# Gate and up products of 18 of 22 tiles by seven products per 2x2 block, in six feed-forward layers on one core

## What is computed

```
def swiglu(h, w1, w3, w2):
    return (jax.nn.silu(h @ w1) * (h @ w3)) @ w2          # 1024 -> 2816 -> 1024
def swiglu_2(h, w_in, w_out):
    gate, up = jnp.split(h @ w_in, 2, axis=-1)            # 1024 -> 2 x 2816 -> 1024
    return (jax.nn.silu(gate) * up) @ w_out
```

## Time and profile before

| | us |
|---|---|
| median of three runs | 2272.77 |
| lowest, highest | 2272.24, 2274.1 |
| the profiled execution, its own time | 2274.54 |
| its span, first to last instruction | 2272.5 |

### The profile page before, as it was taken

The page is one execution under the profiler, slowest core; times in us unless marked ns, Lnnn a source line. Parts: engine busy times, 40 slices in busy tenths (PEclk is TensorE's granted clock), DMA queues, the critical chain, the costliest instruction groups (busy, mean ns, idle before and its releaser), DMA issues.

```text
span 2272.5 us, 23963 instructions
## 1 busy us (share of the span) xinstructions
PE 2211.6 (97%) x10232; PEld 1871.7 (82%) x10232; DVE 766.8 (34%) x1601; ACT 356.2 (16%) x667; POOL 118.8 (5%) x231
## 2 busy tenths in 40 slices
PE   7999999999999999999999999999999999999997
PEld 4777888868888888888788888888888868888886
DVE  6454333313334122336433422332233543340002
ACT  3233200022000100023140200020002223120001
POOL 0100011100111000100000000000010000000000
PEclk9999999999999999999999999999999999999998
DMA  9673576825767565643434465656564433444331
GB/s 357 226 259 102 213 267 245 311 79 186 270 248 295 220 230 199 254 147 146 162 111 148 157 231 200 236 195 231 213 231 154 154 148 111 148 148 148 137 127 70
DMA packets 61539, 438.27 MB, mean 193 GB/s; under 512 B 6976, under 2 KB 8768, under 8 KB 39552
## 3 DMA queue, kind: packets, MB, share of 16 engines
q1 hardware_dynamic: 28608, 318.35, 38.4%
q0 software_dynamic: 32256, 117.45, 13.9%
q10 hardware_dynamic: 576, 1.05, 0.1%
HBM read 434.72 MB, written 2.10 MB: 192 GB/s over the span
## 4 chain that ended last, share of the span: by engine, by line
PE 97%; DVE 1%; ACT 1%; issue 0%; DMA 0%; SPq 0%; ACTq 0%; DVEq 0%
PE lin L1460 79%; PE small_ps L1460 4%; PE lin L1775 2%; PE lin L1718 1%; PE small_ps L1794 1%; PE lin L1528 1%; PE lin L1732 1%; PE small_ps L1564 1%; PE small_ps L1685 1%; PE lin L1672 1%; PE lin L1740 1%; PE small_ps L1766 0%; PE pstat L1472 0%; PE lin L1600 0%; PE small_ps L1615 0%; PE lin L1587 0%
## 5 line engine op out<-in xcount | busy, mean ns | idle before, releaser
L1460 PE MATMUL lin<-h,ring 128*128 128x256 f32 x5424 | 1180.3, 380 | 5.4 <-ACT h L807 2.8
L1460 PEld LDWEIGHTS lin<-h,ring 128*128 128x128 f32 x5424 | 1030.0, 190 | 150.7 <-issue 9.2
L1460 PE MATMUL lin<-big,ring 128*128 128x256 f32 x2112 | 457.4, 379 | 7.9 <-DVE big L1422 7.9
L1460 PEld LDWEIGHTS lin<-big,ring 128*128 128x128 f32 x2112 | 400.8, 190 | 64.5 <-DVE big L1422 10.3
L871 DVE CUSTOM_DVE_ANT_0 ada_ring<-ada_ring,crow 128x1024 f32<-128x1024 f32 x224 | 268.2, 1219 | 26.7 <-DMA ada_ring<-in_ada 26.1
L1422 DVE TENSOR_TENSOR big<-sil,lin 128x256 f32<-128x256 f32 x112 | 47.1, 421 | 592.8 <-ACT sil L835 592.8
L464 POOL DMA_DIRECT2D ada_ring<-in_ada x224 | 118.3, 528 | 1592.9 <-DVE sums L871 1561.0
L1012 DVE SCALAR_TENSOR_TENSOR x<-lin,mod,x 128x256 f32<-128x256 f32 x80 | 38.7, 483 | 449.3 <-PE lin L1460 424.2
L835 ACT ACTIVATE sil<-lin 128x256 f32<-128x256 f32 x112 | 42.9, 383 | 723.2 <-PE lin L1460 723.2
L1460 PE MATMUL lin<-rec,ring 128*128 128x257 f32 (+1 forms) x608 | 148.2, 397 | 7.8 <-ACT rec L532 7.8
L1460 PEld LDWEIGHTS lin<-rec,ring 128*128 128x128 f32 x608 | 120.8, 199 | 28.5 <-issue 9.6
(11 more groups left out here) (296 smaller groups left out, 1175.1 us busy)
## 6 DMA issues: line engine op xcount, KB each, us to landing
ring<-in_w SPq DMA_DIRECT2D x66, 2048.0 KB, 8.3
ada_ring<-in_ada POOLq DMA_DIRECT2D x224, 512.0 KB, 5.6
ring<-in_w SPq DMA_DIRECT2D x48, 1408.0 KB, 6.1
ring<-in_gates SPq DMA_DIRECT2D x12, 2048.0 KB, 7.9
ring<-in_mproj SPq DMA_DIRECT2D x8, 2048.0 KB, 8.0
ring<-in_mtok SPq DMA_DIRECT2D x4, 2048.0 KB, 7.7
ring<-in_branch SPq DMA_DIRECT2D x4, 2048.0 KB, 7.8
ring<-in_wout SPq DMA_DIRECT2D x4, 2048.0 KB, 7.8
```

The lines of the kernel that those rows point to most:

```text
L1460: ins = mm(dst, w[:, lo:lo + m], rhs(k), start=k == 0, stop=k == nk - 1)
```

## The change

The w13 blocks 2 to 10 of each feed-forward layer (nine "chunks", `CHUNKS = 9`) are computed with the Winograd form of Strassen's product. The input is cut in halves of tokens (rows) and of features, `a11 a12 a21 a22`; the chunk's weights in halves of features and in gate and up, `b11 b12 b21 b22`. Seven products of 128 tokens x 512 features x 256 columns, four matmuls each, take the place of eight. Now a part of h (or a sum of parts) is stationary and 256 columns of weights (or of a sum of weights) move; results have tokens on the partitions. The order on TensorE is product 1, 2, [four transposes of the chunk before], 3, 5, 6, 7, 4.

- VectorE makes four sums of h per layer (`combine_h`), four sums of weights per chunk, 128 x 1024 each (`combine`), and nine sums and products of 128 x 256 per chunk out of and into the seven results (`chunk`).
- ScalarE copies product 1 out of PSUM, makes two silus per chunk, and copies the four transposed hidden parts into `big`. These stand in one fixed order.
- TensorE transposes the hidden parts back (`turn_hidden`), the last chunk's behind the first 16 matmuls of w2. The second product of w2 block 0 no longer waits for the last hidden tile as a whole.
- The slot of a chunk is given back after product 5.
- The modulation blocks are shared out anew: 18 of them go ahead of the Fourier mixer's result, 1 to 3 into each chunk.

```
+            def combine(s, j):
...
+                W(t1, b12, b11, ALU.subtract).then_inc(s_weights_combined, 1)
+                W(t3, b22, b12, ALU.subtract).then_inc(s_weights_combined, 1)
+                dve.wait_ge(s_weights_combined, nth(dve, s_weights_combined))
+                W(t2, b22, t1, ALU.subtract).then_inc(s_weights_combined, 1)
+                dve.wait_ge(s_weights_combined, nth(dve, s_weights_combined, 2))
+                W(t4, b21, t2, ALU.subtract).then_inc(s_weights_combined, 1)
...
+            def chunk(s, j):
...
+                dve.wait_ge(s_second_product, nth(dve, s_second_product))
+                dve.wait_ge(s_first_kept, nth(dve, s_first_kept))
+                V.tensor_tensor(first_gate, product_bank(s, 2), first_kept, ALU.add).then_inc(s_first_gate, 1)
+                dve.wait_ge(s_sixth_product, nth(dve, s_sixth_product))
+                added(partial_2, product_bank(s, 6), first_kept)
+                added(first_up, product_bank(s, 5), partial_2, early=j)
+                added(product_bank(s, 3), product_bank(s, 3), first_up, s_first_up)
+                dve.wait_ge(s_first_gate_silu, nth(dve, s_first_gate_silu))
+                V.tensor_tensor(first_up, product_bank(s, 3), first_gate, ALU.mult).then_inc(s_taken_by_dve, 1)
+                dve.wait_ge(s_seventh_product, nth(dve, s_seventh_product))
+                added(partial_3, product_bank(s, 7), partial_2)
+                dve.wait_ge(s_fourth_product, nth(dve, s_fourth_product))
+                V.tensor_tensor(second_gate, product_bank(s, 4), partial_3, ALU.add).then_inc(s_second_gate, 1)
+                added(product_bank(s, 5), product_bank(s, 5), partial_3)
+                dve.wait_ge(s_second_gate_silu, nth(dve, s_second_gate_silu))
+                V.tensor_tensor(second_gate, product_bank(s, 5), second_gate, ALU.mult).then_inc(s_taken_by_dve, 1)
...
+                    ada(ADA_IN_UNITS[ffn])
+                    for j in range(CHUNKS):
+                        chunk(s, j)
+                        if j + 1 < CHUNKS:
+                            combine(s, j + 1)
+                        ada(ADA_IN_CHUNKS[ffn][j])
...
+                    for j in range(CHUNKS + 1):
+                        if j < CHUNKS:
+                            act.wait_ge(s_first_product, nth(act, s_first_product))
+                            if j:
+                                act.wait_ge(s_first_up, nth(act, s_first_up))
+                            A(first_kept, product_bank(s, 1), ACT.Copy).then_inc(s_first_kept, 1)
+                        if j:
+                            act.wait_ge(s_second_gate, nth(act, s_second_gate))
+                            A(second_gate, second_gate, ACT.Silu).then_inc(s_second_gate_silu, 1)
+                            act.wait_ge(s_hidden_turned, nth(act, s_hidden_turned))
+                            at = RAW + 2 * (j - 1)
+                            A(big[:, at:at + 2], pstat[:].rearrange("p (a b) -> p a b", a=2), ACT.Copy).then_inc(s_hidden_kept, 1)
+                        if j < CHUNKS:
+                            act.wait_ge(s_first_gate, nth(act, s_first_gate))
+                            A(first_gate, first_gate, ACT.Silu).then_inc(s_first_gate_silu, 1)
...
+                    part(1, quarter_of_h(0, 0), b11).then_inc(s_first_product, 1)
+                    part(2, quarter_of_h(1, 0), b21).then_inc(s_second_product, 1)
+                    if j:
+                        turn_hidden(j - 1)
+                    part(3, combined_h(3), b22)
+                    if j:
+                        pe.wait_ge(s_second_gate, before + j)
+                    else:
+                        pe.wait_ge(*taken(u0 + RAW - 1))
+                    pe.wait_ge(s_weights_combined, 4 * (before + j + 1))
+                    part(5, combined_h(0), t1).then_inc(s_unit, 2)
+                    part(6, combined_h(1), t2).then_inc(s_sixth_product, 1)
+                    part(7, combined_h(2), t3).then_inc(s_seventh_product, 1)
+                    part(4, quarter_of_h(1, 1), t4).then_inc(s_fourth_product, 1)
...
+                pe.wait_ge(s_first_up, before + CHUNKS)
+                result(0, 16)
+                turn_hidden(last)
+                result(16, KF).then_inc(s_unit, 1)
```

More of the change, by code:

```diff
@@ L62 @@
 ADA_IN_MLA = ADA_N - FIRST_GATE + ADA_N
-ADA_PER_FFN = [48, 48, 32, 32, 32, 0]
+ADA_IN_UNITS = [3, 2, 2, 2, 2, 0]
+ADA_IN_CHUNKS = [[3] * 3 + [2] * 6, [2] * 9, [1] * 9, [2] * 9, [2] * 4 + [1] * 5, [0] * 9]
+ADA_IN_RESULTS = [[3] * 6, [3] * 6, [3] * 6, [2] * 6, [3] * 6, [0] * 6]
+ADA_IN_FOURIER = 18
+ADA_PER_FFN = [a + sum(b) + sum(c) for a, b, c in zip(ADA_IN_UNITS, ADA_IN_CHUNKS, ADA_IN_RESULTS)]
+CHUNKS = KF // 2 - RAW // 2
 SLOTS = 3
@@ L824, in _ @@
                     u0 = unit0[s, "w13"]
-                    for n in range(KF):
+                    f = ffn_before(s)
+                    for n in range(RAW):
                         if n >= 2:
@@ L1564, in turn, with gate_and_up, part, turn_hidden @@
                 return nc.tensor.transpose(dst, src, ident[:])
+            def gate_and_up(s):
+                ph, f = by_name[s, "w13"], ffn_before(s)
+                u0, before = ph.unit0, ffn_before(s) * CHUNKS
+                def part(product, activation, weight):
+                    out = product_bank(s, product).rearrange("p (u f) -> p u f", u=2)
+                    for k in range(4):
+                        ins = mm(out, activation[:, k], weight[:, :, k * P:(k + 1) * P], start=k == 0, stop=k == 3)
+                    return ins
+                def turn_hidden(j):
+                    pe.wait_ge(*taken(u0 + RAW + 2 * j + 1))
+                    if j:
+                        pe.wait_ge(s_hidden_kept, before + j)
+                    for a in range(2):
+                        for tt, tokens in enumerate((first_up, second_gate)):
+                            at = a * T + tt * P
+                            ins = turn(pstat[:, at:at + P], tokens[:, a * P:(a + 1) * P])
+                    ins.then_inc(s_hidden_turned, 1)
+                h_tile(KD - 1)
+                pe.wait_ge(s_h_combined, 4 * (f + 1))
+                for j in range(CHUNKS):
+                    n = ph.first + RAW // 2 + j
+                    slot_of(ph, 0, RAW // 2 + j)
+                    b11, b12, b21, b22 = [quarter(n % SLOTS, c, half) for half in range(2) for c in range(2)]
+                    t1, t2, t3, t4 = [combined_weights(j, i) for i in range(4)]
+                    if j:
+                        pe.wait_ge(s_first_gate, before + j)
+                    else:
+                        pe.wait_ge(*taken(u0 + 2))
+                    part(1, quarter_of_h(0, 0), b11).then_inc(s_first_product, 1)
+                    part(2, quarter_of_h(1, 0), b21).then_inc(s_second_product, 1)
+                    if j:
+                        turn_hidden(j - 1)
+                    part(3, combined_h(3), b22)
+                    if j:
+                        pe.wait_ge(s_second_gate, before + j)
+                    else:
+                        pe.wait_ge(*taken(u0 + RAW - 1))
[4 more added lines that the diff above has]
+                    part(4, quarter_of_h(1, 1), t4).then_inc(s_fourth_product, 1)
+                last = CHUNKS - 1
+                ph = by_name[s, "w2"]
+                w = slot_of(ph, 0, 0)
+                b = bank(ph.unit0)
+                def result(k0, k1):
+                    for k in range(k0, k1):
+                        if k >= RAW and k % 2 == 0:
+                            pe.wait_ge(s_hidden_kept, before + (k - RAW) // 2 + 1)
+                        ins = mm(b[:, 0:T], w[:, k * P:(k + 1) * P], big[:, k], start=k == 0, stop=k == KF - 1)
+                    return ins
+                pe.wait_ge(s_first_up, before + CHUNKS)
+                result(0, 16)
+                turn_hidden(last)
+                result(16, KF).then_inc(s_unit, 1)
@@ L1943, in _ @@
                         raw_unit(ph, r)
[L1944 to L1947, removed]
+                    if not folded(s):
+                        for b in range(RAW // 2):
+                            pairs(ph, b // SLOTS, b % SLOTS, 2, h_tile)
+                    gate_and_up(s)
+                    ph = by_name[s, "w2"]
+                    for m in range(1, KD):
+                        w = slot_of(ph, m // SLOTS, m % SLOTS)
+                        tile_sum(bank(ph.unit0 + m)[:, 0:T], w, 0, KF, lambda k: big[:, k]).then_inc(s_unit, 1)
                 if kind == "mix":
```

90 lines of the change are left out of this document (78 added, 12 removed).

## The result

The changed kernel took 2371.5 us (median of four runs, 2369.8 to 2373.2) against 2273.3 us before: a ratio of 1.043 (95% interval 1.041 to 1.045), so it is 4.3% slower. The forecast was 2370 us.

What follows compares the result with a forecast made beforehand. TensorE, on the chain for 97% of the span, was taken as the bound; +36 us of longer turns and +61 us of lower clock on 2272.8 gave 2370 us, range 2305 to 2396.

Steps and rivals of the forecast that it cites:

- the turn: Chunks, one product 5 to the next, through TensorE, ScalarE and VectorE: 14.88 us, with TensorE standing 2.35 us before product 5.
- TensorE's own price: TensorE's work per chunk, seven products and four transposes: 12.53 us against 13.81, at an unchanged price per matmul.
- The rival that moving weights are slower: Chunk products: matmuls with moving weights 10% slower, turns 0.7 to 1.2 us longer, 2420 us; chance 0.04.
- the one of quick sums: VectorE's four sums of weights take 2.6 us, turn 12.7 us, kernel faster at 2204 us; chance 0.09 with a related case.
- drops of 1.7 us: TensorE's granted clock partly at 1.2 GHz behind stalls before product 5: 36 falls of 1.7 us, +61 us.
- three in four: Assumed share of the 48 stalls before product 5 followed by a clock fall: 36, between none and all.
- The rival in which the clock holds: Stalls before product 5 come but TensorE's clock stays full: 2309 us; chance 0.11.
- What was hidden: Transposes, VectorE's other work, ScalarE's other silu and copy, loads and modulation blocks within a turn: all costed at nothing.
- In the first chunk of each layer: Chunk 0 has its sums ahead of time: ready 1304.8 us, product 5 due 1305.2, no stall by 0.4 us.
- The term "nothing": Eighteen modulation blocks before the Fourier mixer's result: first result perhaps 1 to 2 us late, TensorE's bank needed 10.4 us later.
- 36 + 61: Six layers' longer turns, +36 us, plus clock falls in the chunks, +61 us: +97 us.
- the prediction's pair of 1.10 and 1.55 us: TensorE idle stretches at 1266 in the old trace, one of five such pairs at later second-stack sublayers, each followed by a fall.

Runs made afterwards that it cites:

- experiment 1: Changed kernel with ScalarE's silu of a chunk's second gate ahead of the copy of the next chunk's product 1: 2237.6 us, 0.984 of the kernel before.
- experiment 2: Changed kernel with VectorE's sums of weights made one chunk ahead: 2198.5 us, 0.967 of the kernel before.
- experiment 4: Changed kernel with a fifth, useless sum of 128x1024 ahead of the fourth sum of weights: 2473.8 us, 1.088 of the kernel before.
- experiment 3: Changed kernel with useless matmuls between products 3 and 5 of chunks 1 to 8: 2313.4 us with five, 2310.4 with two, 2310.8 with one.
- experiment 5: Changed kernel with 12 modulation blocks instead of 18 ahead of the Fourier mixer's result: 2368.0 us, 1.041 of the kernel before.

## Why the prediction was right

**The chain.** Every hop of the turn was taken from a row, and the turn came out as 14.93 us where 14.88 stood in the forecast. Counted from product 5: ScalarE began at 8.91 (forecast 8.88), VectorE's product at 9.70 (9.71), the first sum at 10.04 (10.05), the last sum ended at 14.79 (14.82). Three of the terms were off and nearly cancelled: the silu took 0.41 us and not the 0.51 of L830, but ScalarE to VectorE took 0.10 and not 0.04, and VectorE to TensorE 0.14 and not 0.06. Experiments 1, 2 and 4 each pulled one link and moved the time as the chain says.

**TensorE's own price.** 12.53 us a chunk, measured as exactly that in experiment 2. The rival that moving weights are slower is out. So is the one of quick sums, which needed some 0.65 us each: the chain above has them at 1.13 to 1.14 from one to the next and 1.24 for the last.

**The clock.** 35 drops of 1.7 us against a forecast of 36; without them the six layers are 59 us shorter (848.7 - 789.7), where 61 stood in the sum. The mechanism is shown by experiment 3. That the number was so near is partly luck: three in four was a choice between two rows. The rival in which the clock holds would have been 2309 us, and 2310 to 2313 is what the kernel takes when the idle stretch is filled. The rule of the Trainium skill ("TensorE: Matmul & The Clock Gate", section "Why this matters for your kernels") warns only of idle gaps longer than these. It is too lax here: 35 of 48 gaps of 2.17 us brought a drop.

**What was hidden.** The transposes, VectorE's other sums, the modulation blocks in the chunks and the loads cost nothing, as said. In the first chunk of each layer product 5 came without a visible wait.

**What was wrong.** The term "nothing" for the 18 modulation blocks ahead of the Fourier mixer's result. I had put their transfers at some 33 us, three in flight at 5.6 us each; the burst took from 482 to 524, 41 us, since VectorE waited 7.9 us for the last block, and the first results were taken too late for TensorE's banks. It cost 4.3 us (experiment 5), 2.55 of stall and 1.7 of clock. What the term left out is that a block of the ring would be loaded at the same time. That the two slowed each other is read from the landing times, not tried by itself; how much it costs varies: in the profiled execution of experiment 1 the same eighteen blocks were in time by 498.5 us and TensorE did not stand.

**The sum.** Six layers take 141.7, 141.7, 140.0, 142.0, 141.7 and 141.7 us from product 1 to w2, 848.7 together; before, one took 125.6 (the forecast's figure), six 753.8 by their marks. That is +95 (36 of turns and 59 of clock), and with +4.3 around the Fourier mixer +99; the spans differ by 98.6. The forecast had 36 + 61 = +97, so 2 us too many for the clock made up for a part of the 4.3 us that were missing.

## What to carry to other kernels

Ask of every new product on the busiest engine what it waits for, and follow that back through the order of each queue, not only through the data: here a silu stood behind a copy that belonged to the next round, and the sums stood behind the silu, so a saving of 1.3 us a chunk became a loss of 1.1. If operands can be made a round ahead, in a second buffer that is there already, put their making ahead of the work that waits. Where TensorE must idle over and over, look at the granted clock behind each stall; some useless matmuls there can be worth more than they cost.

## What the runs showed of the hardware that I had not expected

- Whether an idle stretch costs clock is not settled by its length alone. In the chunks 48 stretches of about 1.74 us brought no drop and 48 of about 2.17 us brought 35. But the stretch of 1.92 to 1.93 us ahead of layer 4, after which the kernel before kept its clock, is in all ten traces, and in three of them (experiments 3 with five and with two matmuls, and 4) a drop followed: 0.79 in the mean of 8 us. In experiment 2 one of 1.95 us brought one (0.76 in the mean of 494 to 501). And the prediction's pair of 1.10 and 1.55 us, with 0.7 of work between, had brought one five times.
- Stalls of 3.4 us brought 44 drops in 48, and in 12 of 38 turns with a drop it cost 2.9 us instead of 1.7.
- ScalarE's silu of 128x256 from SBUF took 0.41 us here (L909, mean 409 ns) and 0.51 in the raw units, where it also reads a bias column; that the column makes the difference was not tried.
